# Second attention: each tile's probabilities scaled by the row's reciprocal on GpSimd, ahead of the transposes

## The chip, the cores and the metric

One core of one Trainium2 chip. The metric is the device time of the whole kernel in microseconds (us), median over runs. Before the change it is 2228.61 us (three runs, 2228.41 to 2229.06).

## The reference, cut to what matters

The kernel computes two transformer blocks of two layers each over 512 latent rows (and 256 context rows in the first block). The change touches one stage, the multi-head latent attention of the first block's second layer:

```python
s = (jnp.einsum('bqhd,bkhd->bhqk', qn_b, kn_all)
     + jnp.einsum('bqhr,bkr->bhqk', qr_b, kr_all)).astype(jnp.float32) * scale
p = jax.nn.softmax(s, axis=-1).astype(dt)
return jnp.einsum('bhqk,bkhd->bqhd', p, v_all)
...
y = (o * jax.nn.silu(g)) @ w_o
```

There are 16 heads, 512 queries, 768 keys (512 latent and 256 context), 96 numbers per query and key and 64 per value. The softmax divides each query's exponentials by their sum. That division can be made on the probabilities, or on the output after the product with the values.

## The kernel before, in words

Everything is float32. A projection's operands are split in a high and a low part and cost three products (L365 to L367, split_product). The programs of the five engines are written out by hand; they meet at semaphores: Signal.mark numbers an instruction's increment, and wait_ge on the same key waits for it. Each engine runs its program in the order written, so an instruction that waits holds everything behind it on its engine.

**The attention's steps.** ATT_B (L1213) has 16 jobs, one per head, of four tiles of 128 queries by 768 keys: 64 tiles. A step t of the loops att_pe, att_dve, att_act and att_pool handles tile t, and the later work of earlier tiles. Within step t:
- TensorE (att_pe, L656) makes the scores of tile t (six products, L543, into two of four PSUM banks; it first waits for the exponential of tile t-2, which read those banks), then transposes the probabilities of tile t-2 (six, L615, in two lots of three, each into one of three turning banks), then prep_pe (up-projections of a later head's keys and queries), then its share of the value products of a finished pair of heads (L651), then, once per pair, the spread (below).
- VectorE (att_dve, L673) takes the negated row maximum of tile t (L553), copies the first lot of transposes of tile t-2 from PSUM to PT (L633), makes the reciprocals of a pair (L584), the pair's output (keep_o, b_keep, L1050), and the low parts of a later head's keys and queries (prep_dve: L1150, L1156, L1159, and for some heads rope products L820 to L829).
- ScalarE (att_act, L692) copies the second lot of tile t-2 (L635), makes the exponential of tile t with its row sums (L568, into PB and SUM), then high parts.
- GpSimd (att_pool, L711) gates a pair (L720, below) and makes the high and low parts of finished outputs (b_parts_pool, L1063: a cast L1068 and a subtraction L1070 per pair of heads). These stand at three steps only, named by pairs_at (L1220): pairs 0 and 1 at tile 3 of head 13, pairs 2 and 3 at tile 3 of head 14, pairs 4 to 6 at tile 2 of head 15. At the last pair's spread step, low_at, it first makes the low parts of three weight panels (split_low, L1481).

**How a pair is placed.** finish_att (L788) counts from z, the last tile of an odd head: its reciprocals at z+2, its spread at z+3, its value products in four shares at z+3 to z+6, its output at z+7 (for the last pair all value products at z+3, the output at z+4).

**The normalization before the change.** The probabilities stay unnormalized. att_spread (L586) multiplies each reciprocal column, broadcast, with the identity, so that the reciprocals of a pair lie along the free dimension of a PSUM bank (8 products, L594, recorded as 16). ScalarE copies that to BC (L604). GpSimd multiplies the gate by BC (L720, `gated`), and VectorE's output (L1053) is the value product times that gate; it waits for `gated`.

The steps have different lengths, since only some carry the extra work. I call a pair's even head e and its odd head o, with tiles 0 to 3: e2, e3, o0 and o1 are long (value products, up-projections), o2, o3, e0 and e1 are short (scores and transposes alone). Lines above are those of the kernel before.

## Time and profile before

| | |
|---|---|
| median of 3 runs | 2228.61 us |
| span of the profiled execution | 2224.4 us |
| the profiled execution's own time | not given apart from its span; the runs lie 4.2 us above the span |
| TensorE matmuls busy over the span | 94% |
| VectorE, ScalarE, GpSimd busy over the span | 47%, 40%, 34% |
| mean granted TensorE clock | 0.971 of full |
| the second attention | about 592 us to 808 us of the span |

The span runs from the first to the last instruction. Busy shares are means over stages with different limits. In a timeline row the first number is the start (us from the span's start), the second the duration, and brackets at the end tell how long the engine was idle before and what ended it. In --lines style rows the numbers behind the bar are the busy time of the group (us) and the mean of one (ns), then the idle time before them. TensorE's clock has two levels, 2.4 GHz (1.00) and 1.2 GHz (0.50).

### The profile page before, as it was taken

The page shows a single profiled execution, that of the slowest core. Times are in us where ns is not written, and L with a number is a line of the kernel's source. Part 1 is how long each engine was busy: PE and PEld are TensorE (multiplying, and loading weights), DVE is VectorE, ACT ScalarE, POOL GpSimd, SP SyncE. Part 2 cuts the span into 40 slices and gives each one's busy share as a digit, 9 for nine tenths or more (in the row PEclk, how much of TensorE's full clock was granted, in tenths as well). Part 3 has the DMA queues.
Part 4 walks back from the last instruction along what each step waited for, and adds up shares of the span by engine and source line. Part 5 has one row for each costly group of instructions (what it writes and reads, how often), then busy time and mean ns, then how long its engine had stood idle before and what let it go on. Part 6 is the DMA issues. An engine that isn't in the chain of part 4 may idle for free.

```text
span 2224.4 us, 30049 instructions
## 1 busy us (share of the span) xinstructions
PE 2087.9 (94%) x11530; PEld 1654.5 (74%) x11530; DVE 1040.3 (47%) x1723; ACT 891.2 (40%) x1645; POOL 755.4 (34%) x446
## 2 busy tenths in 40 slices
PE   5999999999999999998889999998998889999997
PEld 4888655788666667986667888886986677888886
DVE  3520887422466632388337344333127625625253
ACT  4322666423566643535433222234127633322222
POOL 1331122343000153330344444453445453444443
PEclk9999999999999999799899999999999999999999
DMA  7221333132000012220122333332321132333332
GB/s 284 67 65 57 108 96 96 48 104 67 19 1 1 1 58 76 58 85 20 53 70 86 104 95 95 95 95 76 94 87 39 28 96 60 102 96 98 100 92 69
DMA packets 255890, 169.17 MB, mean 76 GB/s; under 512 B 5776, under 2 KB 247159, under 8 KB 254599
## 3 DMA queue, kind: packets, MB, share of 16 engines
q1 hardware_dynamic: 252512, 158.55, 24.0%
q0 software_dynamic: 2192, 8.45, 1.2%
q8 instruction: 94, 1.54, 0.3%
q10 hardware_dynamic: 1047, 0.26, 0.1%
q14 instruction: 45, 0.37, 0.1%
HBM read 165.10 MB, written 2.14 MB: 75 GB/s over the span
## 4 chain that ended last, share of the span: by engine, by line
PE 82%; DVE 8%; issue 4%; ACT 3%; POOL 1%; DMA 0%; ACTq 0%; DVEq 0%; POOLq 0%
PE ps L365 21%; PE ps L366 20%; PE ps L367 20%; PE ps L543 6%; PE ps L651 5%; PE ps L615 3%; PE ps L594 1%; DVE MX L556 1%; DVE PT L633 1%; POOL WL L1481 1%; PE ps L516 1%; DVE NB L553 1%; PE ps L987 1%; ACT PB L568 1%; PE ps L1086 1%
## 5 line engine op out<-in xcount | busy, mean ns | idle before, releaser
L1481 POOL TENSOR_TENSOR WL<-raww,WH 128x1024 fp32r<-128x1024 f32 (+2 forms) x247 | 581.8, 2360 | 894.2 <-ACT WH L317 882.7
L365 PE MATMUL ps<-HH,WH 128*128 128x512 f32 (+1 forms) x1368 | 526.0, 384 | 29.1 <-DVE HL L486 17.0
L366 PE MATMUL ps<-HL,WH 128*128 128x512 f32 (+1 forms) x1368 | 520.7, 381 | 0.0
L367 PE MATMUL ps<-HH,WL 128*128 128x512 f32 (+1 forms) x1368 | 519.7, 380 | 0.0
L317 ACT ACTIVATE WH<-raww 128x1024 fp32r<-128x1024 f32 (+2 forms) x247 | 254.2, 1035 | 327.7 <-PE ps L367 327.6
L365 PEld LDWEIGHTS ps<-HH,WH 128*128 128x128 f32 x1368 | 260.9, 191 | 88.8 <-issue 29.9
L367 PEld LDWEIGHTS ps<-HH,WL 128*128 128x128 f32 x1368 | 260.4, 190 | 49.3
L366 PEld LDWEIGHTS ps<-HL,WH 128*128 128x128 f32 x1368 | 261.0, 191 | 46.6
L568 ACT ACTIVATE PB<-ps,NB 128x256 f32<-128x256 f32 (+5 forms) x256 | 167.8, 656 | 101.8 <-DVE NB L557 51.9
L615 PE MATMUL ps<-ident,PB 128*128 128x128 f32 x952 | 154.5, 278 | 11.6 <-DVE PT L633 7.1
L651 PE MATMUL ps<-PT,ARENA 128*64 128x512 f32 (+3 forms) x688 | 132.8, 493 | 11.2 <-ACT PT L635 7.8
L365 PE MATMUL ps<-f_h,WH 128*128 128x512 f32 x352 | 137.7, 391 | 1.6 <-DVE f_l L2605 1.6
L367 PE MATMUL ps<-f_h,WL 128*128 128x512 f32 x352 | 137.1, 389 | 0.0
L366 PE MATMUL ps<-f_l,WH 128*128 128x512 f32 x352 | 137.0, 389 | 0.0
L553 DVE TENSOR_REDUCE NB<-ps 128x1 f32<-128x768 f32 (+4 forms) x128 | 92.5, 722 | 94.5 <-PE ps L543 92.8
L615 PEld LDWEIGHTS ps<-ident,PB 128*128 128x128 f32 x952 | 108.7, 142 | 22.0 <-DVE PT L633 12.6
L635 ACT ACTIVATE PT<-ps 128x256 f32<-128x256 f32 (+1 forms) x192 | 83.5, 435 | 90.3 <-PE ps L615 88.2
L2418 DVE TENSOR_TENSOR ARENA<-ps,ARENA 128x512 f32<-128x512 f32 x60 | 40.8, 689 | 157.8 <-PE ps L367 131.1
L2592 DVE SCALAR_TENSOR_TENSOR ARENA<-ARENA,COL 128x511 f32<-128x511 f32 x44 | 110.8, 2518 | 1.6
L2181 ACT ACTIVATE ARENA<-ARENA 128x512 f32<-128x512 f32 x44 | 27.9, 633 | 172.9 <-DVE ARENA L2594 172.9
L556 DVE TENSOR_REDUCE MX<-ps 128x1 f32<-128x512 f32 (+3 forms) x128 | 74.0, 578 | 42.0 <-PE ps L543 41.5
L633 DVE COPY PT<-ps 128x384 f32<-128x384 f32 (+2 forms) x192 | 91.2, 475 | 3.2 <-PE ps L615 2.1
(330 smaller groups left out, 3392.0 us busy)
## 6 DMA issues: line engine op xcount, KB each, us to landing
raww<-in_ffn_w_up SPq DMA_DIRECT2D x88, 512.0 KB, 3.8
raww<-in_ada_w SPq DMA_DIRECT2D x32, 512.0 KB, 3.6
raww<-in_ffn_w_down SPq DMA_DIRECT2D x32, 448.0 KB, 3.7
raww<-in_odd_w_in SPq DMA_DIRECT2D x24, 512.0 KB, 3.7
raww<-in_even_w_in SPq DMA_DIRECT2D x21, 512.0 KB, 3.7
raww<-in_a_w_in SPq DMA_DIRECT2D x20, 512.0 KB, 3.8
raww<-in_ffn_w_down SPq DMA_DIRECT2D x16, 512.0 KB, 3.8
ADA<-in_ada_w SPq DMA_DIRECT2D x6, 1024.0 KB, 16.9
```

The lines of the kernel that those rows point to most:

```text
L317: nc.scalar.activation(parts_of(k)[0], raw_slot(k), ACT.Copy).then_inc(*split_hi.mark(k))
L365: nc.tensor.matmul(out, lh, rh, start=start and k == ks[0], stop=False)
L366: nc.tensor.matmul(out, lh, rl, start=False, stop=False)
L367: ins = nc.tensor.matmul(out, ll, rh, start=False, stop=stop and k == ks[-1])
L543: ins = nc.tensor.matmul(ps[:, bk, c0 % 512:c0 % 512 + w], lhs, rhs, start=(q == 0), stop=(q == len(ms) - 1), skip_group_check=True)
L553: nc.vector.tensor_reduce(nb, score_span(A, r, i), AX_X, ALU.max, negate=True)\
L568: nc.scalar.activation(PB[:, t % 4, 0:job["tiles"][i]["n"] * P], score_span(A, r, i), ACT.Exp, bias=NB[:, r % 4, i:i + 1], scale=A["scale" ...
L615: ins = nc.tensor.transpose(ps[:, b, q * P:(q + 1) * P], PB[:, t % 4, (first + q) * P:(first + q + 1) * P], ident[:, :])
L633: nc.vector.tensor_copy(dst, src).then_inc(*pt_dve.mark(*key))
L651: ins = nc.tensor.matmul(ps[p0:p0 + HD, 7, a:z], v, PT[at][:, blk, q0_ + a:q0_ + z], start=(q == 0), stop=(q == n - 1), skip_group_check=True)
L1481: nc.gpsimd.tensor_tensor(lo, raw_slot(k), hi.bitcast(F32), ALU.subtract).then_inc(*split_lo.mark(k))
L2592: chain(dve, dve_step, nc.vector.scalar_tensor_tensor(c[:, 1:S], u[:, 0:S - 1], col(cw, 22 + m), c[:, 1:S], ALU.mult, ALU.add))
```

## The change

For ATT_B alone ("weigh": True), in four parts. VectorE makes one reciprocal of 128x1 per tile (tile_rcp), in the step after the tile's own, right behind that step's maximum. GpSimd multiplies the tile's probabilities in PB, 128x768, in place by that column (tile_weigh), first in its step. TensorE's transposes of the tile wait for that product (`weighed`) instead of the exponential. The pair reciprocals, the spread products, their copy to BC and the gate's multiplication are left out, and b_keep no longer waits for `gated`. The split_low of the last spread step stays, and pairs_at is unchanged.

```diff
+        def tile_rcp(dve, A, r, i):
+            dve.wait_ge(*exp_made[A["name"], r, i])
+            nc.vector.reciprocal(RCP[:, r % 4, i:i + 1], SUM[:, r % 4, i:i + 1])\
+                .then_inc(*rcp_made.mark(A["name"], r, i))
+
+        def tile_weigh(pool, A, r, i):
+            t = A["at"](r, i)
+            p = PB[:, t % 4, 0:A["jobs"][r]["tiles"][i]["n"] * P]
+            pool.wait_ge(*rcp_made[A["name"], r, i])
+            nc.gpsimd.tensor_scalar(p, p, RCP[:, r % 4, i:i + 1], None, ALU.mult)\
+                .then_inc(*weighed.mark(A["name"], r, i))
...
         def att_turn(pe, A, r, i):
             t = A["at"](r, i)
-            pe.wait_ge(*exp_made[A["name"], r, i])
+            pe.wait_ge(*(weighed if "weigh" in A else exp_made)[A["name"], r, i])
...
-                if t in A["spread_at"]:
+                if t in A["spread_at"] and "weigh" not in A:
                     att_spread(pe, A, A["spread_at"][t])
...
                 if r is not None:
                     att_max(dve, A, r, i)
+                if "weigh" in A and att_at(A, t - 1)[0] is not None:
+                    tile_rcp(dve, A, *att_at(A, t - 1))
                 q, j = att_at(A, t - 2)
                 if q is not None:
                     att_keep("dve", A, q, j)
-                if t in A["rcp_at"]:
+                if t in A["rcp_at"] and "weigh" not in A:
                     att_rcp(dve, A, A["rcp_at"][t])
...
-                if t in A["spread_at"]:
+                if t in A["spread_at"] and "weigh" not in A:
                     att_spread_keep(act, A, A["spread_at"][t])
...
         def att_pool(pool, A):
             for t in range(A["steps"]):
+                if "weigh" in A and att_at(A, t - 1)[0] is not None:
+                    tile_weigh(pool, A, *att_at(A, t - 1))
                 if t in A["spread_at"]:
...
                         split_low(pool, A["low_at"][t])
+                if t in A["spread_at"] and "weigh" not in A:
                     pool.wait_ge(*bc_made[A["name"], q])
...
         def b_keep(dve, job, r):
             g = b_gate(job)
-            dve.wait_ge(*gated["B", r])
...
-        ATT_B = finish_att({"name": "B", "jobs": b_jobs(), "scale": 1.0, "keep_o": b_keep, "gate": b_gate,
+        ATT_B = finish_att({"name": "B", "weigh": True, "jobs": b_jobs(), "scale": 1.0, "keep_o": b_keep, "gate": b_gate,
```

## Rows read from the trace of the kernel before

**Rows 1.** The page's part 1: busy time, share of the span, instructions.

```profile
PE 2087.9 (94%) x11530; PEld 1654.5 (74%) x11530; DVE 1040.3 (47%) x1723; ACT 891.2 (40%) x1645; POOL 755.4 (34%) x446
```

**Rows 2.** Windows, second attention: length; PE, PEld, DVE, ACT, POOL busy (instructions); PEclk; DMA share, GB/s.

```profile
590.00:816.00 226.00, 211.01 (x1193) 139.10 (x1192) 139.01 (x213) 144.56 (x283) 30.34 (x25) 0.99 0.03 8
```

**Rows 3.** Waits, 620 to 830 us: who waited for whom, total us, times, longest.

```profile
PE ps L543 <- DVE b_ql L1159: 5.2, 6, 0.9
...
DVE ARENA L1053 <- POOL ARENA L720: 11.5, 1, 11.5
```

**Rows 4.** Groups by line and shape, 592 to 808.3 us, TensorE and ScalarE.

```profile
L594 PE MATMUL ps<-ident,RCP 128*64 128x128 f32 x128 | 8.6, 275 | 0.0
...
L568 ACT ACTIVATE PB<-ps,NB 128x768 f32<-128x768 f32 x64 | 57.5, 898 | 15.2 <-DVE NB L553 14.7
...
L568 ACT ACTIVATION_READ_ACCUMULATOR PB<-ps,NB 128x1 f32 x64 | 12.6, 198 | 0.0
```

**Rows 5.** Timeline of TensorE, 740 to 760 us: the steps o3 to e3 of one pair.

```profile
745.77 0.48 PE L543 MATMUL ps<-b_kk,b_qh 96*128 96x512 f32 x1
...
748.60 0.47 PE L543 MATMUL ps<-b_kk,b_qh 96*128 96x512 f32 x1 [0.87 <-DVE b_ql L1159]
...
749.74 0.82 PE L615 MATMUL ps<-ident,PB 128*128 128x128 f32 x6
750.61 0.47 PE L543 MATMUL ps<-b_kk,b_qh 96*128 96x512 f32 x1
...
752.32 0.48 PE L543 MATMUL ps<-b_kk,b_qh 96*128 96x512 f32 x1
...
753.46 0.82 PE L615 MATMUL ps<-ident,PB 128*128 128x128 f32 x6
...
755.98 1.04 PE L594 MATMUL ps<-ident,RCP 128*64 128x128 f32 x16
756.96 0.50 PE L543 MATMUL ps<-b_kk,b_qh 96*128 96x512 f32 x1
```

**Rows 6.** Timeline of VectorE, 740 to 757 us.

```profile
748.49 0.96 DVE L553 TENSOR_REDUCE NB<-ps 128x1 f32<-128x768 f32 x1
...
751.95 0.96 DVE L553 TENSOR_REDUCE NB<-ps 128x1 f32<-128x768 f32 x1 [0.59 <-PE ps L543]
...
753.28 0.19 DVE L584 RECIPROCAL RCP<-SUM 128x8 f32<-128x8 f32 x1
753.51 0.95 DVE L1150 TENSOR_TENSOR b_kk<-ARENA,b_kk 64x768 fp32r<-64x768 f32 x1
```

**Rows 7.** Groups by line and shape of GpSimd, whole span.

```profile
L379 POOL TENSOR_TENSOR ACC<-ACC,SQ 128x768 f32<-128x768 f32 x5 | 9.2, 1846 | 20.7 <-ACT SQ L396 20.7
L1070 POOL TENSOR_TENSOR b_ol<-ARENA,b_oh 128x512 fp32r<-128x512 f32 x7 | 8.9, 1276 | 0.6
...
L1068 POOL CAST b_oh<-ARENA 128x512 fp32r<-128x512 f32 x7 | 4.3, 610 | 9.1 <-issue 5.6 <-DVE ARENA L1053 3.2
L959 POOL CAST a_oh<-ARENA 128x256 fp32r<-128x256 f32 x7 | 2.8, 396 | 34.8 <-DVE ARENA L937 30.0 <-DVE MROW L1015 4.8
```

**Rows 8.** GpSimd's casts of L1303: shortest, median and longest duration in ns.

```profile
L1303 POOL CAST o_oh<-OT x7: 609/1055/1055, 1686.9 to 1772.2; 128x512 fp32r<-128x512 f32 x7
```

**Rows 9.** Timeline, 786 to 830 us: the attention's end, all engines.

```profile
790.31 1.94 PE L651 MATMUL ps<-PT,ARENA 128*64 128x512 f32 x8
...
792.17 0.50 PE L543 MATMUL ps<-b_kk,b_qh 96*128 96x512 f32 x1
...
800.36 7.07 PE L651 MATMUL ps<-PT,ARENA 128*64 128x512 f32 x24 [1.86 <-ACT PT L635]
...
808.23 0.50 PE L365 MATMUL ps<-b_oh,WH 128*128 128x512 f32 x1
```

**Rows 10.** Windows of 2 us, TensorE alone: length, busy (instructions), granted clock, DMA share, GB/s.

```profile
798.00:800.00 2.00, 0.50 (x5) 1.00 0.00 0
...
802.00:804.00 2.00, 2.00 (x7) 0.50 0.76 223
```

More of the change, by code:

```diff
@@ L189, in build @@
             scores_made turned pv_made max_made exp_made sink_made rcp_made
-            pt_dve pt_act o_made spread_made bc_made gated summed act_step dve_step pool_step const_made""".split()
+            weighed pt_dve pt_act o_made spread_made bc_made gated summed act_step dve_step pool_step const_made""".split()
         sg = {n: signal(n) for n in names}
@@ L193, in build @@
          pool_out, squared, rms_made, diag_made, h_made, x_made, scores_made, turned,
-         pv_made, max_made, exp_made, sink_made, rcp_made, pt_dve, pt_act, o_made,
+         pv_made, max_made, exp_made, sink_made, rcp_made, weighed, pt_dve, pt_act, o_made,
          spread_made, bc_made, gated, summed,
```

## The prediction

> **What bounds the kernel now.** I read the page's busy shares first: TensorE is busy 94% of the span and no other engine half of it [rows 1]. Then the windows of the second attention: TensorE is busy 211 of 226 us, VectorE and ScalarE about 140, GpSimd 30, at a clock of 0.99 [rows 2]. So the stage is TensorE's queue, with GpSimd nearly free. The waits show the exceptions: six times TensorE waits 0.9 us for VectorE's low parts of the next head (5.2 us together), and once, at the end, VectorE waits 11.5 us for GpSimd's gate [rows 3]. The timeline of TensorE then gives the steps of one pair: o3 starts at 745.77, e0 at 748.60, e1 at 750.61, e2 at 752.32, e3 at 756.96 [rows 5]. The question is whether the new chain (maximum, reciprocal, GpSimd, transpose) fits in short steps: o3 to e0 is 2.8 us, e0 to e1 2.0, e1 to e2 1.7, and only e2 to e3 is long, 4.6.
>
> **What is removed.** The spread is 128 recorded products, one group per pair; a group holds TensorE from 755.98 to 756.96, 0.98 us [rows 4, 5]. Eight groups are 7.8 us, all on TensorE's path. The copy to BC and the gate's multiplication go too; ScalarE and GpSimd had room for them, so I take nothing for that. The 11.5 us wait at the end frees nothing: TensorE went straight on to the output projection at 808.23 and did not wait for that output [rows 3, 9].
>
> **What one weighing costs.** No row shows GpSimd multiplying by a column. Below stands its cast, one stream in and one out: 396 ns for 256 elements and 610 ns for 512, so 0.836 ns an element and 182 ns fixed, 0.82 us for 768. Above stands its two-input addition of 128x768, 1.85 us [rows 7]. The multiplication also reads one stream, so I stay near the cast and take 1.0 us. Each hand-over between engines I take as 0.1 us, and the reciprocal, by the 128x8 one, from its start at 753.28 to the next instruction at 753.51, as 0.2 us [rows 6]. In all 64 weighings add 64 us of GpSimd to 30; it does not become a full engine. Latency is the matter.
>
> The Trainium skill, GPSIMD Engine Reference, section Engine selection, says to keep elementwise work on VectorE, with one-input work on GpSimd "roughly line-rate"; the casts' 0.836 ns an element agree. Its section Elementwise — side-by-side cycle accounting gives 1.8 cycles an element at 1.2 GHz for a tight loop, an estimate of 1.15 us for 768; by that the sum below would be 3 us more.
>
> **One transition of pairs, worked out on the rows.** In o2 VectorE now has a reciprocal more (0.2), and its low parts with two operands from memory meet a weighing (I take 0.2 more; one-sided slowdowns of that sort are seen on GpSimd, 609 against 1055 ns for one cast [rows 8]). e0 was released by those low parts, so it starts at 749.0 instead of 748.60, and the maximum of tile o3 at 748.9, ending at 749.85. Only behind it comes the reciprocal of tile o2, to 750.0; GpSimd weighs 750.15 to 751.15; the transposes of o2 start at 751.25. TensorE would be ready 1.14 us after its scores started (748.60 to 749.74 [rows 5]), at 750.14: a stall of 1.1 us. e1 starts 0.57 later, at 751.8, and was at 750.61. Tile o3's weighing is ready at 752.7, TensorE at 752.95: no stall. e2 starts at 753.5. The maximum of e1 starts 1.34 us after its scores (750.61 to 751.95 [rows 5, 6]), 753.15, ends 754.1; reciprocal of e0 to 754.25; weighing to 755.4; transposes at 755.5, while TensorE is ready at 754.65: a stall of 0.85. From these transposes to e3 it was 3.5 us (753.46 to 756.96), without the spread 2.5: e3 starts at 758.0 instead of 756.96. The long steps e3, o0, o1 have over 3.5 us, in which the chain fits. So one transition, with its spread already taken off, is 1.05 us longer. The exponential is not the end of the chain: 0.90 plus 0.20 us behind a maximum [rows 4] is done before the next tile's maximum is. Three of the seven transitions also hold rope work on VectorE ahead of a maximum; the same steps give 1.5 there. Sum: 4 x 1.05 + 3 x 1.5 = 8.7 us. The head of the attention adds 0.3.
>
> **The casts that stand before weighings.** GpSimd's high and low parts, 610 + 1276 ns and gaps, are 2.0 us a pair of heads [rows 7]. They used to run in an idle engine; now the next tile's weighing is queued behind them, and TensorE's transposes behind that. Two pairs at tile 3 of head 13: the weighing of that tile ends 4.1 us later, in a short step: 3.4 us of stall instead of 0.9, plus 2.5. Two pairs at tile 3 of head 14, in long steps: plus 1.0. Three pairs at tile 2 of head 15, last steps: tile 62's weighing starts 9.7 us after step 62's scores, 6.1 of them the casts; transposes of 62 at 10.8 and of 63 at 11.9; then ScalarE's weight copy and its last lot, value products at about 13.6, where before they started 8.2 us after 792.17 (at 800.36) [rows 9]. That is 5.4 later, less the last spread, 1.0: plus 4.4.
>
> **The clock.** The end of the attention shows what a hole does: TensorE busy 0.50 of 2 us at 798, then the granted clock at 0.50 (1.2 GHz) at 802 [rows 10]. One fall there cost 1.3 us: the 24 value products took 7.07 us, where 8 undisturbed ones take 1.94 [rows 9], so 5.8 for 24. The new hole of 3.4 us should cost the same; the one of about 6 us starts the fall that is there already earlier and lets it catch more, for which I take 1.0: plus 2.3.
>
> **Sum.** 8.7 + 0.3 + 2.5 + 1.0 + 4.4 + 2.3 = 19.2 us on a span of 2224.4, so 2243.6; the median of the runs, 2228.6, lies 4.2 above the span, so 2248. Per microsecond of weighing the sum moves by 19 (two stalls in each of seven transitions, and the ends): the cast's 0.82 gives 15.8 and 2244, the addition's 1.85 gives 35.4 and 2264.
>
> **Rivals.**
> - **The weighing hides and the spreads are a gain.** For it: GpSimd idles and 7.8 us of TensorE work go. It needs stalls below the spread, which by the slope of 2 per transition means a weighing under 0.5 us, less than GpSimd's own cast of 512 elements [rows 7]. If the reciprocals also overlapped the maxima, 7.8 us less: 2221. Decides at the transposes of o2 and e0: no idle before them. Chance 0.05; that both just cancel, 2228.6, also 0.05.
> - **GpSimd multiplies at the pace of its two-input addition**, 1.85 us: 2264. For it: that is the only arithmetic of this size in the rows. Chance 0.10.
> - **VectorE and GpSimd hold each other up.** Four low-part instructions with two operands in memory lie in each head; the cast that goes from 609 to 1055 ns [rows 8] shows 0.45 us. On every weighing that is 0.45 x 19 = 8.5 us more: 2256.5. Chance 0.08. The Trainium skill, SBUF — State Buffer, section Who interferes with whom, says that the second of two such instructions fully blocks until the first ends, not that both slow; by that rule only the weighings that start second pay, which is nearer to my 0.2.
> - **The clock falls in every transition**, not at the two holes alone. There TensorE would idle some 2.5 us in about 8. At 1.3 us a fall, as above, 7 x 1.3 = 9 more, 2257. Against it: the same stretch today has stalls of 0.9 and the stage's clock is 0.99 [rows 2]. Chance 0.10.
>
> **How the numbers follow.** My forecast has 0.62. I give 2248 with 2236 to 2267: the low end is the cast's price (15.8) without the clock's losses (2.3), the casts' delays in head 13 and 14 (3.5) and half of the end's cost (2.2), the high end is just past the addition's price. About 0.2% (4.5 us) is what a measurement here tells from no change. Faster 0.05, within 0.05, slower 0.90.
>
> **What would show it.** Right: the weighing's mean near 1.0 us; TensorE idle before L615-type transposes, released by GpSimd, about twice per transition and near 1 us each, 25 us in all with 3 us at head 13's last tile and 6 us at the end; the stage from 216 to about 235 us, all other stages unchanged. Wrong: a weighing outside 0.8 to 1.9 us; releases by GpSimd in the long steps as well; a gap at the end under 3 us; or a difference in any stage outside 592 to 830 us.

## The result, and the profile after

The changed kernel takes 2278.4 us (median of 4 runs, 2265.2 to 2279.1) against 2228.5 for the kernel before in the same batch: a ratio of 1.0215 [1.0201, 1.0229]. The direction was right and the size was not: 49.9 us slower where 19.4 were forecast, and outside the range. The changed kernel has two levels of time, 2265 and some 2278; the profiled execution is the single one at 2265 (span 2263.4), and experiment 11 below shows where the other 12 us lie.

The page's part 1 of the changed kernel answers [rows 1]: GpSimd has 131 us more, TensorE 5 us more although 128 products are gone.

```profile
PE 2092.6 (92%) x11402; PEld 1653.0 (73%) x11402; DVE 1064.1 (47%) x1779; ACT 888.0 (39%) x1637; POOL 886.8 (39%) x502
```

The stage first. I measure the second attention from its first score product to the first product of its output projection: 592.28 to 808.23 before, 595.80 to 859.40 after. These are the windows of the changed kernel (length; PE, PEld, DVE, ACT, POOL busy; granted clock), first the attention, then a stretch of the next layer's row products:

```profile
595.80:859.40 263.60, 215.02 (x1029) 140.08 (x1029) 158.39 (x262) 136.73 (x268) 160.97 (x81) 0.88 0.02 7
946.00:976.00 30.00, 30.00 (x257) 30.00 (x257) 15.28 (x17) 20.08 (x35) 9.92 (x4) 1.00 0.29 86
```

The same window of the kernel before (592.28 to 808.23) is 215.95 us long with TensorE busy for 202.13, at a clock of 0.99 ([rows 2] is the same stretch with some us on each side). So the attention is 47.6 us longer. Everything ahead of it is 3.5 us longer and everything behind it 12.2 us shorter in this profile, both of which vary from execution to execution of these kernels as well. Read TensorE's column: busy 202.1 became 215.0, and idle (length less busy) 13.8 became 48.6. Of the busy time the spreads took 7.8, so the same products cost 20.7 us more than before, at a mean clock of 0.88 instead of 0.99. The account of the stage is then **34.8 us of new idle time, 20.7 us by which products take longer at the lower clock, 7.8 us of spreads gone**: 47.7. It is an account of TensorE's time and not yet of causes: a product that runs slower can fill what would otherwise be a wait.

The weighing itself, from the groups by line (busy us, mean ns, idle before), and the waits from 590 to 870 us (total us, times, longest):

```profile
L596 POOL TENSOR_SCALAR PB<-PB,RCP 128x768 f32<-128x768 f32 x64 | 141.0, 2205 | 128.2 <-DVE RCP L588 127.8
```

```profile
POOL PB L596 <- DVE RCP L588: 127.8, 56, 33.3
...
PE ps L628 <- POOL PB L596: 46.8, 30, 7.4
```

The multiplication takes 2.2 us, more than the highest bound of the forecast. And nearly all of TensorE's idle time, 46.8 of 48.6 us, ends with GpSimd's weighing; before, the waits were other and smaller ones [rows 3].

TensorE's timeline of one pair transition, heads 9 to 10, from the scores of tile o3 at 741.13. It is one of the three with rope work:

```profile
741.13 0.48 PE L543 MATMUL ps<-b_kk,b_qh 96*128 96x512 f32 x1
...
744.14 1.53 PE L628 MATMUL ps<-ident,PB 128*128 128x128 f32 x6 [1.72 <-POOL PB L596]
...
747.90 0.88 PE L628 MATMUL ps<-ident,PB 128*128 128x128 f32 x6 [0.31 <-POOL PB L596]
...
751.11 0.87 PE L628 MATMUL ps<-ident,PB 128*128 128x128 f32 x6 [1.28 <-POOL PB L596]
...
753.71 0.87 PE L628 MATMUL ps<-ident,PB 128*128 128x128 f32 x6 [0.68 <-POOL PB L596]
```

Four transposes in a row wait, where I expected two. The first of them also runs at 1.2 GHz: six transposes in 1.53 us, against 0.88. The transition of [rows 5], heads 11 to 12, has no rope work. In the changed kernel its o3 starts at 770.76:

```profile
770.76 0.47 PE L543 MATMUL ps<-b_kk,b_qh 96*128 96x512 f32 x1
...
773.77 0.87 PE L628 MATMUL ps<-ident,PB 128*128 128x128 f32 x6 [1.73 <-POOL PB L596]
...
777.40 1.54 PE L628 MATMUL ps<-ident,PB 128*128 128x128 f32 x6 [1.16 <-POOL PB L596]
...
784.28 0.87 PE L628 MATMUL ps<-ident,PB 128*128 128x128 f32 x6 [1.23 <-POOL PB L596]
```

The waits of the transposes of o2 and e0 are there, 1.16 and 1.23 us where the forecast had 1.1 and 0.85, and so is the forecast's free passage of o3. The new one, 1.73 us, is that of tile o1: its transposes stand in step o3, but its reciprocal comes behind the maximum of o2, and step o2 is short. From o3 to e3 the transition takes 16.20 us instead of 11.19. GpSimd in the stretch of the first view (start, duration, idle before) has no gap as long as a weighing:

```profile
745.64 2.20 POOL L596 TENSOR_SCALAR PB<-PB,RCP 128x768 f32<-128x768 f32 x1 [1.55 <-DVE RCP L588]
748.85 2.20 POOL L596 TENSOR_SCALAR PB<-PB,RCP 128x768 f32<-128x768 f32 x1 [1.01 <-DVE RCP L588]
751.45 2.21 POOL L596 TENSOR_SCALAR PB<-PB,RCP 128x768 f32<-128x768 f32 x1 [0.40 <-DVE RCP L588]
```

The loop reads off: a weighing ends (747.84), the transposes start (747.90), the scores behind them follow (748.54), their maximum comes behind rope work in VectorE's queue and runs to 751.3, the reciprocal behind it frees the weighing at 751.45, the second after the one that the loop began with. The engines take turns where they used to overlap.

The end of the attention, TensorE only, answers [rows 9]:

```profile
814.31 1.54 PE L628 MATMUL ps<-ident,PB 128*128 128x128 f32 x6 [2.78 <-POOL PB L596]
...
831.33 0.87 PE L628 MATMUL ps<-ident,PB 128*128 128x128 f32 x6 [3.12 <-POOL PB L596]
...
846.99 1.54 PE L628 MATMUL ps<-ident,PB 128*128 128x128 f32 x6 [7.38 <-POOL PB L596]
849.17 1.54 PE L628 MATMUL ps<-ident,PB 128*128 128x128 f32 x6 [0.64 <-POOL PB L596]
851.39 8.05 PE L664 MATMUL ps<-PT,ARENA 128*64 128x512 f32 x24 [0.67 <-ACT PT L648]
859.37 0.50 PE L365 MATMUL ps<-b_oh,WH 128*128 128x512 f32 x1
```

There are three holes behind casts: 2.8 us at head 13's last tile (forecast 3.4), 3.1 at head 14's last tile, where the forecast had only 1.0 more, and 7.4 at the end (forecast about 6). The last 24 value products run at the lower clock again, 8.05 us.

The length of the attention by place, from the starts of the scores in TensorE's timelines (us more than in the kernel before; runs 3 and 5 are described below):

| place | forecast | run 3, weighing 1.24 us | run 5, 2.20 us, holes filled | changed kernel |
|---|---|---|---|---|
| first scores to o3 of head 1 | 0.3 | 0.4 | 2.7 | 4.7 |
| six transitions, o3 to e3, heads 1 to 12 | 7.65 | 4.9 | 17.7 | 21.9 |
| the stretches between them, e3 to o3 | 0 | -0.1 | -0.1 | -0.1 |
| o3 of head 13 to the output projection | 11.25 | 10.6 | 20.4 | 21.1 |
| sum | 19.2 | 15.8 | 40.7 | 47.6 |

So the loss lies where the forecast put it, and the long steps take part in none of it.

### The profile page after: what moved, and what is told of

Its sections match the earlier page's. It is cut to its first block, busy times and chain, and to the rows that moved or that the text cites. A ratio compares the mean times of both kernels' runs of the same rounds, so it can differ in the third digit from the quotient of the medians.

```text
span 2263.4 us, 29870 instructions
## 1 busy us (share of the span) xinstructions
PE 2092.6 (92%) x11402; PEld 1653.0 (73%) x11402; DVE 1064.1 (47%) x1779; ACT 888.0 (39%) x1637; POOL 886.8 (39%) x502
## 4 chain that ended last, share of the span: by engine, by line
PE 80%; DVE 8%; issue 5%; POOL 4%; ACT 3%; DMA 0%; ACTq 0%; DVEq 0%; POOLq 0%
PE ps L365 20%; PE ps L366 20%; PE ps L367 20%; PE ps L543 6%; PE ps L664 5%; PE ps L628 3%; POOL PB L596 2%; DVE MX L556 1%; PE ps L607 1%; DVE NB L553 1%; POOL WL L1498 1%; DVE PT L646 1%; PE ps L516 1%; PE ps L1005 1%; PE ps L1103 1%
## 5 line engine op out<-in xcount | busy, mean ns | idle before, releaser
L628 PE MATMUL ps<-ident,PB 128*128 128x128 f32 x952 | 164.7, 293 | 54.5 <-POOL PB L596 46.8
L596 POOL TENSOR_SCALAR PB<-PB,RCP 128x768 f32<-128x768 f32 x64 | 141.0, 2205 | 128.2 <-DVE RCP L588 127.8
L628 PEld LDWEIGHTS ps<-ident,PB 128*128 128x128 f32 x952 | 114.6, 150 | 70.9 <-POOL PB L596 53.8
L646 DVE COPY PT<-ps 128x384 f32<-128x384 f32 (+2 forms) x192 | 91.1, 475 | 22.8 <-PE ps L628 21.5
```

The lines of the kernel that those rows point to most:

```text
L596: nc.gpsimd.tensor_scalar(p, p, RCP[:, r % 4, i:i + 1], None, ALU.mult)\
L628: ins = nc.tensor.transpose(ps[:, b, q * P:(q + 1) * P], PB[:, t % 4, (first + q) * P:(first + q + 1) * P], ident[:, :])
L646: nc.vector.tensor_copy(dst, src).then_inc(*pt_dve.mark(*key))
```

## Experiments

Runs of one batch share the runs of the kernel before (2227.2 to 2228.5), and each ratio is against those. For the attention alone I give, from the window of each profile, its length, TensorE's busy and idle time, and the granted clock.

**1. The price alone.** The kernel before, with five GpSimd instructions added at its very end, on 256, 512 and 768 elements, one after the other.

```
+            for n in (256, 512, 768):
...
+                        ins = nc.gpsimd.tensor_copy(o, x)
...
+                        ins = nc.gpsimd.tensor_scalar(o, x, c, None, ALU.mult)
...
+                        ins = nc.gpsimd.tensor_scalar(o, x, 0.5, None, ALU.mult)
...
+                        ins = nc.gpsimd.tensor_tensor(o, x, c.to_broadcast([P, n]), ALU.mult)
...
+                        ins = nc.gpsimd.tensor_tensor(o, x, BENCH[:, 0:n], ALU.mult)
```

> The kernel before, with five GpSimd operations on idle memory added behind its last work, each waited for before the next, at 256, 512 and 768 elements: cast-like copy, multiplication by a column, multiplication by a constant, product with a broadcast column, product of two tiles. Theory L (the operation itself is slow): the column multiplication of 768 takes 2.2 us here too, with VectorE nearly idle. Rival C (VectorE held it up in the attention): here it takes under 1.3 us, near the copy's 0.8. If the constant's form is fast and the column's slow, it is the column operand that costs.

2236.7 us in one run. The timeline of GpSimd; the other engines are still at work up to 2224.2 and done behind it:

```profile
2212.20 0.93 POOL L1481 TENSOR_SCALAR BENCH<-BENCH,RCP 128x256 f32<-128x256 f32 x1
...
2216.23 1.56 POOL L1481 TENSOR_SCALAR BENCH<-BENCH,RCP 128x512 f32<-128x512 f32 x1
...
2224.99 2.20 POOL L1481 TENSOR_SCALAR BENCH<-BENCH,RCP 128x768 f32<-128x768 f32 x1
2227.28 2.13 POOL L1483 TENSOR_SCALAR BENCH<-BENCH 128x768 f32<-128x768 f32 x1
2229.49 1.47 POOL L1485 TENSOR_TENSOR BENCH<-BENCH,RCP 128x768 f32<-128x768 f32 x1
2231.04 1.47 POOL L1487 TENSOR_TENSOR BENCH<-BENCH 128x768 f32<-128x768 f32 x1
```

So 2.2 us is the operation's own price: it is the same with VectorE idle, and nearly the same with a constant in the place of the column. It grows by 2.48 ns an element ((2.20 - 0.93) us / 512), the cast by 0.84 [rows 7]. That VectorE makes it dear is refuted. The form with two inputs, one of them the column repeated, is a third cheaper, 1.47 us. Three of the fifteen instructions are out of line: the constant on 512 elements 2.15 us (2.13 on 768), the product of a tile with itself on 512 1.90 (1.47 on 768), the copy of 768 1.70 (0.61 for 512). All three ran beside VectorE's last four products of two operands in memory, here from 2217.39 to 2224.21, so VectorE can hold GpSimd up, though the two-input form on 512 ran there undisturbed (1.04 us); it does not do so to the weighing, which takes 2.20 us in the kernel too.

**2. Neither the spreads nor the weighing**: the normalization is left out altogether.

```
-            pe.wait_ge(*(weighed if "weigh" in A else exp_made)[A["name"], r, i])
+            pe.wait_ge(*exp_made[A["name"], r, i])
...
-                    tile_rcp(dve, A, *att_at(A, t - 1))
...
-                    tile_weigh(pool, A, *att_at(A, t - 1))
```

> The changed kernel without weighing and without tile reciprocals: transposes wait for the exponential, and nothing normalizes the probabilities (that division is left out). What the removal alone is worth. Theory L: the eight spreads' 7.8 us of TensorE come off in full, 2221. Rival: part of them covered waits of other engines, and under 4 us come off, 2225 or more.

2222.3 us (9 runs), 0.9977 [0.9967, 0.9987]. Attention 209.3, busy 194.4, idle 14.8, clock 0.99. What the change removes is worth 5.0 us in the time and 6.7 in the stage, of the 7.8 forecast. So the new chain costs 54.3 us of stage in the changed kernel.

**3 and 4. The same chain with a shorter weighing**: only 384 or only 32 of each row's 768 probabilities are multiplied; the rest stays unnormalized.

```
-            p = PB[:, t % 4, 0:A["jobs"][r]["tiles"][i]["n"] * P]
+            p = PB[:, t % 4, 0:3 * P]        (run 3)
+            p = PB[:, t % 4, 0:32]           (run 4)
```

> The changed kernel, weighing only the first 384 of 768 columns (the other half stays unnormalized). The weighing should take about 1.2 us instead of 2.2. Theory L with 19 us per us of weighing: 19 us off, about 2259 from 2278, and most idle time before the transposes goes. Rival K (the granted clock's falls make most of the loss): it stays above 2268 as long as holes are there at all.

> The changed kernel, weighing 32 of 768 columns: the same chain of engines with an operation of about 0.25 us. Theory L: no stall in the transitions, the casts in front of weighings still cost some us; 7.8 us of spreads are gone, so 2224 to 2232. Rival H (the hand-overs and the place behind the maximum cost as much as the multiplication): 2240 or more.

Run 3: 2245.6 (5 runs, 2232 to 2249), 1.0071 [1.0047, 1.0095]. That is 33 us off where 19 were expected: more than the weighing's slope comes back. Run 4: 2232.2 (10 runs), 1.0024 [1.0015, 1.0034], at the upper end of what was expected. First the group and the waits of run 3, then those of run 4:

```profile
L596 POOL TENSOR_SCALAR PB<-PB,RCP 128x384 f32<-128x384 f32 x64 | 79.6, 1244 | 160.4 <-DVE RCP L588 160.1
```

```profile
PE ps L628 <- POOL PB L596: 31.6, 28, 6.4
```

```profile
L596 POOL TENSOR_SCALAR PB<-PB,RCP 128x32 f32<-128x32 f32 x64 | 23.2, 363 | 202.3 <-DVE RCP L588 202.0
```

```profile
PE ps L628 <- POOL PB L596: 13.5, 12, 5.5
```

| weighing, us | attention | TensorE busy | TensorE idle | clock |
|---|---|---|---|---|
| none (run 2) | 209.3 | 194.4 | 14.8 | 0.99 |
| 0.36 (run 4) | 221.1 | 199.3 | 21.7 | 0.97 |
| 1.24 (run 3) | 231.8 | 198.1 | 33.7 | 0.98 |
| 2.20 (changed kernel) | 263.6 | 215.0 | 48.6 | 0.88 |

The idle column is nearly a straight line: 13.6 us per us of weighing from 0.36 to 1.24 ((33.7 - 21.7) / 0.88), 15.5 from there to 2.20 ((48.6 - 33.7) / 0.96). The busy column is flat up to 1.24 us and then jumps by 17. The length, which is what counts, does not follow one slope: 12 us per us of weighing up to 1.24, 33 from there. The profile of run 3 is of its quickest execution (2232); like the changed kernel's it has the clock at 1.00 in the next layer's row products, and the 11 to 16 us to its other runs fit the 12.5 of run 11 below; none of those was profiled.

**5. Is it the clock?** The holes of the changed kernel are filled: ahead of the wait for the weighing, in four of the eight steps of a pair, TensorE transposes the identity 8 times into the bank that it is about to use.

```
-            pe.wait_ge(*(weighed if "weigh" in A else exp_made)[A["name"], r, i])
...
+                if g == 0 and "weigh" in A and (r % 2, i) in ((1, 1), (1, 2), (1, 3), (0, 0)):
+                    for q in range(8):
+                        nc.tensor.transpose(ps[:, b, (q % 4) * P:(q % 4 + 1) * P], ident[:, :], ident[:, :])
+                if g == 0:
+                    pe.wait_ge(*(weighed if "weigh" in A else exp_made)[A["name"], r, i])
```

> The changed kernel, and TensorE fills its holes: for the tiles whose transposes stand in short steps (o1, o2, o3, e0) it makes eight transposes of the identity into the same bank before it waits for the weighed tile. 256 transposes of about 0.11 us more work. Theory K (the holes make the granted clock fall, and the falls cost as much as the holes): the time at 0.50 inside the attention, 54 us in the changed kernel, falls below 20, and the attention gets shorter than 263.6 us by 5 or more in spite of the added work. Theory L alone (the clock's falls lie in waiting time and cost little): 263.6 us or more.

2267.6 us (4 runs), 1.0184 [1.0169, 1.0199], 10.8 below the changed kernel. Its attention:

```profile
591.40:848.10 256.70, 225.85 (x1284) 155.28 (x1284) 158.26 (x262) 136.53 (x268) 160.77 (x81) 0.97 0.02 5
```

TensorE does 256 transposes more, and the attention is 6.9 us shorter. The clock is 0.97 instead of 0.88: worked out from these means, some 15 us at the lower level instead of 63. The 256 are 34.2 us by their group; that leaves 191.7 for the kernel's own products, no more than in runs 2 to 4. So the jump of 17 us in busy time is the clock's, and it came from the holes. In length it is worth 6.9 us and not 17, since products that run slower fill waits. The transition shown above can be compared with the same one in the second profile of the changed kernel (run 11), where the clock did not fall in it:

```profile
740.74 0.87 PE L628 MATMUL ps<-ident,PB 128*128 128x128 f32 x6 [1.71 <-POOL PB L596]
...
744.49 0.87 PE L628 MATMUL ps<-ident,PB 128*128 128x128 f32 x6 [1.84 <-POOL PB L596]
...
747.71 0.87 PE L628 MATMUL ps<-ident,PB 128*128 128x128 f32 x6 [1.31 <-POOL PB L596]
...
750.30 0.87 PE L628 MATMUL ps<-ident,PB 128*128 128x128 f32 x6 [0.67 <-POOL PB L596]
```

With the fall the second wait is 0.31 us instead of 1.84, and from o3 to e3 it is 15.26 us with it and 15.25 without. In the transitions without rope work a fall cost more or less by where it came: heads 11 to 12 take 16.20 us with one and 14.66 in run 5, heads 7 to 8 take 14.69 with one.

**6. The cheaper form of the same multiplication.**

```
-            nc.gpsimd.tensor_scalar(p, p, RCP[:, r % 4, i:i + 1], None, ALU.mult)
+            nc.gpsimd.tensor_tensor(p, p, RCP[:, r % 4, i:i + 1].to_broadcast([P, 6 * P]), ALU.mult)
```

> The changed kernel, the weighing written as a two-input product with the reciprocal column broadcast, which took 1.47 us for 768 elements where the column multiplication took 2.20 (measured alone at the kernel's end). Theory L, by the run with 384 columns (1.24 us, 2246): 1.5 us should give 2248 to 2258. Rival C (two reading streams meet VectorE's two-input operations): the operation takes 1.8 us or more in the attention and the time stays above 2262.

2257.7 us (4 runs, 2253 to 2265), 1.0138 [1.0117, 1.0160]; the weighing takes 1466 ns, as in run 1. Attention 249.8, busy 206.5, idle 43.3, clock 0.94. Of 20.8 us gained by the median, 13.8 show in this profile's attention (the profile is of the slowest of the four runs). The idle time fell by 5.3 only, not by 0.74 x 15.5 = 11.5. VectorE's busy time in the stage rose from 158.4 to 171.5 with the same 262 instructions: here the two-input form did slow VectorE. How much of the gain that took is not measured.

**7. The casts spread out**: GpSimd's high and low parts, one pair per step instead of two or three.

```
-        ATT_B["pairs_at"] = {ATT_B["at"](13, 3): (0, 1), ATT_B["at"](14, 3): (2, 3), ATT_B["at"](15, 2): (4, 5, 6)}
+        ATT_B["pairs_at"] = {ATT_B["at"](13, 1): (0,), ATT_B["at"](13, 2): (1,), ATT_B["at"](14, 0): (2,),
+                             ATT_B["at"](14, 2): (3,), ATT_B["at"](15, 0): (4,), ATT_B["at"](15, 1): (5,), ATT_B["at"](15, 3) + 1: (6,)}
```

> The changed kernel with the output casts of the seven pairs spread: one pair each at tiles 1 and 2 of head 13, 0 and 2 of head 14, 0 and 1 of head 15, the last behind the last weighing. The prediction put 7.9 us on their old places (2.5, 1.0, 4.4) and 2.3 on the clock there: 7 to 12 us off, about 2268 of 2278, and no gap over 4 us before the last transposes. Rival: the gaps move into other steps and less than 3 us come off.

2253.7 us (4 runs, 2250 to 2264), 1.0125 [1.0099, 1.0151]. Attention 255.5, idle 42.4, clock 0.91. The waits from 595 to 850 us:

```profile
PE ps L628 <- POOL PB L596: 40.6, 30, 2.5
```

As many waits, 30, the longest 2.5 us instead of 7.4. The stage is 8.1 us shorter, and 9.3 from o3 of head 13 on, where the casts were; the forecast had 7.9 for the casts (2.5 + 1.0 + 4.4) and 2.3 for the clock at the same holes. This step of the prediction holds in its sum. The median fell by 24.7, more than that; its profile shows no stretch at the lower clock in the next layer's row products, unlike the level at 2278, so about 12 us of the 24.7 belong to that (run 11).

**8. Another place for the factor.** VectorE multiplies the identity by the reciprocal (128x128) and TensorE transposes by a product with that diagonal; GpSimd does nothing.

```
+            nc.vector.tensor_scalar(DIAG[:, A["at"](r, i) % 3, :], ident[:, :], RCP[:, r % 4, i:i + 1], None, ALU.mult)\
+                .then_inc(*weighed.mark(A["name"], r, i))
...
+                    if "weigh" in A:
+                        ins = nc.tensor.matmul(ps[:, b, q * P:(q + 1) * P],
+                                               PB[:, t % 4, (first + q) * P:(first + q + 1) * P], DIAG[:, t % 3, :],
+                                               start=True, stop=True)
+                        continue
```

> Normalization at no width: VectorE makes the reciprocal and then a 128x128 diagonal of it (identity times the column), and TensorE turns each block by a product with that diagonal instead of a transpose. No spread, no weighing, no gate product, GpSimd free again. Theory L: the chain behind the maximum is two short VectorE operations, 0.3 to 0.4 us, no stall before the turns; the spreads' 5 to 7 us come off, 0.2 to 0.4 us per head come back on VectorE: 2222 to 2228. Rival H (any work between the exponential and the transpose costs more than the spread): above 2232. If a real product with 128x128 is slower than a transpose, the 384 turns show it.

2255.2 us (4 runs), 1.0128 [1.0111, 1.0145]. The stalls are gone: idle 7.5 us, half of run 2's, clock 1.00. But TensorE's busy time is 234.7, 40.2 more than in run 2. Groups by line:

```profile
L592 DVE TENSOR_SCALAR DIAG<-ident,RCP 128x128 f32<-128x128 f32 x64 | 20.4, 319 | 2.3
...
L633 PE MATMUL ps<-DIAG,PB 128*128 128x128 f32 x768 | 97.2, 276 | 4.0 <-DVE DIAG L592 3.6
```

There are 768 records for 384 products: a true fp32 product is recorded twice where a transpose is recorded once, and costs about twice. That the latency makes the stalls is right, but this way out is dear: against the changed kernel the attention is 21.4 us shorter, against the kernel before 26.2 longer. The 2222 to 2228 that I expected missed the price of the product.

**9. More distance.** The transposes and the copies behind them come three steps after the scores instead of two (there are four buffers of probabilities).

```
-                q, j = att_at(A, t - 2)
+                q, j = att_at(A, t - A.get("lag", 2))        ("lag": 3 in the second attention)
```

> The changed kernel with one line of distance more: transposes and their copies of tile t-3 instead of t-2 in step t, value products and outputs one step later. The weighing (2.2 us) and the casts' places are as changed. Theory L (the loss is the latency between a maximum and the transposes two steps on): with a third step the chain, 2.33 + 0.3 + 2.2 + 0.1 us, fits in two steps of 3.7 us or more, short of 1.2 us here and there; the transition stalls mostly go, the casts' and the end's stay: 2235 to 2250. Rival M (GpSimd's amount of work, not its place, is the limit, 141 us of weighing and 20 of casts and panels in a stage of 216): the loss stays near the changed kernel's, above 2262.

2239.5 us (4 runs), 1.0059 [1.0046, 1.0072]. Attention 228.7, busy 203.2, idle 25.4, clock 0.95. The waits of the stage:

```profile
PE ps L628 <- POOL PB L596: 12.5, 6, 6.5
```

GpSimd does the same 64 weighings at 2.2 us (busy 162.9), and TensorE waits for them 6 times instead of 30. So the amount of GpSimd's work never was the matter, its place in the chain was.

**10. All three together**: 6, 7 and 9.

> As the run before, with the weighing as a product with the broadcast column (1.47 us) and the casts one pair at a time. Theory L: no stall left in the transitions, some 3 us more at the end, the spreads' 5 to 7 us off: 2222 to 2230, so level with the kernel before or just under it. Rival M: 2240 or more.

2233.6 us (12 runs, 2224 to 2237), 1.0025 [1.0015, 1.0036], above the 2222 to 2230 expected. Attention 223.4, idle 20.9, clock 0.97. What TensorE waits for now:

```profile
PE ps L628 <- DVE PT L646: 11.0, 12, 1.7
...
PE ps L628 <- POOL PB L596: 2.2, 3, 1.1
```

The weighing is hidden, and the next engine shows itself: VectorE, whose copies of the transposed probabilities come late behind the maximum and the reciprocal, at 174.6 us busy of 223.4.

**11. The changed kernel once more**, for a profile of its other level.

> The changed kernel once more. Its four runs were 2265.2 and three near 2278.5. Theory G: the 13 us are the granted clock in the stretch of the next layer's row products, 75 to 125 us behind the attention: in the profiled 2265 it stayed at 1.00, in the kernel before it is at 0.50 for 23.9 us. If this run is near 2278, its profile shows about 24 us at 0.50 there and the rest of the kernel behind the attention takes 1416 us, if near 2265, none and 1404.

2274.5 us in one run. Its windows, against the two of the section above:

```profile
592.80:856.00 263.20, 214.15 (x1028) 139.16 (x1028) 158.93 (x262) 136.51 (x268) 160.79 (x81) 0.90 0.02 6
944.00:974.00 30.00, 30.00 (x175) 30.00 (x175) 12.00 (x16) 9.17 (x16) 4.74 (x2) 0.65 0.17 51
```

The attention is the same to 0.4 us. Behind it, TensorE is busy all of the 30 us in both profiles, but does 175 products here and 257 there, at a clock of 0.65 against 1.00. What follows the attention takes 1416.5 us here and 1404.0 there; before it took 1416.2, with the lower clock in that stretch too (0.72 from 900 to 930). So 12.5 us of the difference between profiles lie outside the attention. The profiles of these experiments are of the same two kinds: behind the attention come 1404 us in three of them (the changed kernel, runs 3 and 7) and 1415 to 1417 in runs 2, 4 to 6, 8 to 14 and the kernel before. Why the clock stays low there in most executions and not in all, no run shows.

**12. The multiplication on VectorE**, behind the reciprocal, and nothing on GpSimd.

```
-            nc.gpsimd.tensor_scalar(p, p, RCP[:, r % 4, i:i + 1], None, ALU.mult)
+            nc.vector.tensor_scalar(p, p, RCP[:, r % 4, i:i + 1], None, ALU.mult)
```

> The changed kernel with the weighing on VectorE, behind the tile's reciprocal: one 128x768 multiplication by a column, about 0.5 to 0.9 us (a 128x128 one took 0.29). GpSimd is free, no casts in the way. Theory L: 0.9 us against 2.2 less one hand-over removes most stalls in front of transposes, but VectorE gets 64 x 0.7 = 45 us more in its queue, which sets the start of e0 and the rope pairs: 2232 to 2245, far under the changed kernel's 2278.

2234.7 us (8 runs, 2232 to 2248), 1.0048 [1.0029, 1.0066]. Group by line:

```profile
L596 DVE TENSOR_SCALAR PB<-PB,RCP 128x768 f32<-128x768 f32 x64 | 43.9, 687 | 2.3
```

VectorE does in 0.69 us what takes GpSimd 2.20. The profile is of an execution at 2248 (attention 236.0, busy 211.2, idle 24.8, clock 0.93); which stretch those at 2232 save was not profiled. It shows that the sum of idle time does not set the clock: with 24.8 us of it the clock is at 0.93 here, with 33.7 in run 3 and 28.9 in run 14 it is at 0.98. With nothing else altered the median is 43.8 us faster than the changed kernel, though its 43.9 us stand on the busier engine.

**13. Run 10 with the copies first**: on VectorE the copy of the transposed tile goes ahead of the reciprocal.

> As the run with the third step, the broadcast product and the casts apart (2233.6), with one order turned on VectorE: the copy of the turned lot stands before the tile's reciprocal. Theory W (what is left there is a new wait: 20 us in which TensorE waits before transposes for VectorE's copy of the lot before, which now stands behind a maximum and a reciprocal): most of these waits shrink by the 0.2 us of the reciprocal or more, 2 to 4 us off, 2229 to 2232. Rival: the copy waits for the same maximum as before, the weighing comes 0.5 us later, and the time stays or rises, 2233 to 2238.

2232.4 us (10 runs, 2220 to 2238), 1.0009 [0.9992, 1.0027], level with the kernel before. That is 1.2 us under run 10, between what the theory and the rival asked for, and decides nothing. The waits for VectorE's copies fell from 11.0 to 6.3, those for GpSimd rose from 2.2 to 4.8, as the order of the two says.

**14. Run 12 with the third step of distance.**

> The third step of distance, with the weighing on VectorE (0.69 us each, 44 us more in its queue) and GpSimd free. If latency before the transposes was what was left of the loss in the run with the weighing on VectorE (stalls of 23 us there, 2234.7), it goes: 2224 to 2229, level with the kernel before or under it. If VectorE's queue itself is the new bound (it sets the start of e0, the copies and the maxima), the time stays at 2231 or more.

2242.4 us (6 runs, 2231 to 2244), 1.0057 [1.0039, 1.0076], no better than run 12: what was expected if VectorE's queue is the new bound. The waits from 590 to 840 us:

```profile
PE ps L628 <- DVE PT L646: 22.8, 26, 2.6
```

With the weighing in VectorE's queue the copies wait behind it, whatever the distance. None of these versions beats the kernel before except run 2, which leaves the work out.

## Why the prediction was wrong

**What held.** The stage and its bound; that the removed spreads are a gain (6.7 of 7.8 us in the stage); that the matter is the latency of a chain and not GpSimd's sum of work (run 9: same work, 35 us less); the places, with nothing lost in the long steps; that the casts queued ahead of weighings cost some 8 us, though head 14's hole was dearer than forecast (3.1 us of wait) and head 13's cheaper (2.8); and that nothing outside the attention changes: before and behind it the profiles differ by what executions of one kernel differ by (run 11). The sign of being wrong that the prediction named came true, a weighing outside 0.8 to 1.9 us.

**The step that failed** is the price of the weighing: "The multiplication also reads one stream, so I stay near the cast and take 1.0 us." It is 2.205 us in the kernel and 2.20 alone (run 1), above both bounds. The reasoning by streams picked the wrong neighbour twice: the cast at 0.82 us was no lower neighbour but another operation, and the two-input addition at 1.85 was no upper bound: multiplying by a scalar is slower on GpSimd than a product of two inputs (2.20 against 1.47). The Trainium skill, GPSIMD Engine Reference, section Engine selection, says that one-input work is roughly line-rate on GpSimd; this case's traces agree for casts (0.84 ns an element) and not for multiplying by a scalar (2.48 ns an element). The rival at the two-input pace had the mechanism of the result, with 1.85 us, and fell 14 us short. By the prediction's own slope the missing 1.2 us are 22.8: 42.0 us in the stage instead of 19.2.

**The second mis-sized term is the clock.** 2.3 us were forecast, for the two holes at the end, and none for the head and the transitions. There the clock did fall, in five of the six transitions of the changed kernel's profile. Run 5 gives what that costs, 6.9 us (4.2 in the transitions, 2.0 in the head, 0.7 behind): with the holes filled the clock is at 0.97 and the stage that much shorter despite 256 products more. The 20.7 us by which the products take longer are not the cost, since most of them run in what would be waits. The rival "the clock falls in every transition" had this mechanism, and 9 us for it. The argument against it was "the same stretch today has stalls of 0.9", and with stalls near 1 us (run 3, the longest in the six transitions 1.3) the clock does stay up. But it is no matter of the waits' length alone. In the changed kernel the falls came with waits of 1.7 us and up to four in a row, yet the transition of heads 7 to 8 fell at its first wait, that of heads 5 to 6 kept its clock with 1.70, 1.84, 1.31 and 0.69 us, and the one shown under run 5 fell in one execution and not in the other. What decides between them stays open.

**The slope was right on the average, and that is partly luck.** In the six transitions it is 2 us per us of weighing in the forecast; measured, 1.6 each from 0.36 to 1.24 us and 2.2 from there to 2.20 with the clock kept up (68.2, 76.7 and 89.5 us in runs 4, 3 and 5). At its own price the sum was too high: interpolated between runs 4 and 3, a weighing of 1.0 us would have given about 2242, an estimate, where 2248 was forecast. The transitions with rope work, put at 1.5 us, took 0.5 to 0.7 more than before in run 3. The forecast also missed that the transposes of o1 wait ("The long steps e3, o0, o1 have over 3.5 us, in which the chain fits"); that wait is 0.75 us in run 3 and takes the place of one of 0.87 that TensorE had for VectorE's low parts [rows 5].

**Together**, for the stage: forecast 19.2; price 1.2 x 19 = +22.8; the clock beyond the two holes of the forecast, +6.9; rest -1.3, from the slope that was too steep at first. That is 47.6. The median missed by 30.4 and the stage by 28.4; the 2 us between them are less than what the attention's start moves between executions (591 to 596 us).

**The other rivals.** "The weighing hides" needed under 0.5 us. Run 4, at 0.36, is 1.0024 over the kernel before, but in the six transitions it takes 68.2 us where the kernel before takes 71.9: there the weighing nearly hides (65.9 us in run 2) and the spreads are a gain. Of the 11.8 us of stage over run 2, 9.4 lie behind o3 of head 13, where the casts stand ahead of the weighings. "VectorE and GpSimd hold each other up" is refuted as a cost of the weighing (2.20 alone). Its count of four low-part instructions with two operands in each head is not what the rows say either: there are two and a cast, 16 of each. In the other direction it shows: VectorE's cast of 32x512, 0.42 us before, takes 0.90 and 1.01 beside weighings.

```profile
743.46 0.90 DVE L1176 CAST b_ql<-b_rl 32x512 fp32r<-32x512 f32 x1
...
755.87 1.01 DVE L1176 CAST b_ql<-b_rl 32x512 fp32r<-32x512 f32 x1
```

It is 23 us of VectorE's busy time in all (158.4 against 135.1, reciprocals of 10 us among it). The Trainium skill, SBUF — State Buffer, section Who interferes with whom, has one such instruction block until the other ends. For the casts the trace agrees: all 15 that start during a weighing end 0.26 to 0.28 us behind its end, however late they started, so they wait and are not slowed. VectorE's two-operand low parts do not wait for that end: those held up end 1.70 us (64x768) and 1.44 us (64x512) after the weighing's start. In run 6, where the weighing has two inputs, they do: those that start during a weighing end 0.80 and 0.54 us behind its end (means 1.79 and 1.37 us instead of 1.24 and 0.82), and the casts then come when the weighing is over and take 0.42 us.

## What to carry to other kernels

Price an operation on GpSimd by the same operation, not by one that reads as many streams: if no row shows it, the range must reach to several times the nearest one, and one instruction on an idle engine settles it. A new link in a chain that TensorE takes turns with costs its duration once per step in which there is no slack. Distance cures it (one more step between scores and transposes gave back 35 of 48 us of the stage, 39 of the median), and so does a shorter link (on VectorE 44 of the median, run 12); the two did not add up (run 14). For each step, ask which tile's link hangs on the step's end, as o1's hung on the short step o2. Stalls can bring the clock down too, but what slower products cost is read from the length of a stage, not from the engine's busy time: part of them runs in waits.

## What the runs showed of the hardware

On GpSimd, fp32, 128 partitions (run 1): multiplying 256, 512 and 768 elements by a column took 0.93, 1.56 and 2.20 us; the same result as a two-input product with the column broadcast 0.61, 1.04 and 1.47; a constant is hardly cheaper than a column (2.13). VectorE does the 768 in 0.69 (run 12). A GpSimd multiplication by a column holds VectorE's casts up to its own end, a GpSimd product of two inputs holds VectorE's two-operand instructions up to its end (changed kernel and run 6). VectorE's two-operand products held up GpSimd: its copy of 768 elements took 1.70 us beside them (run 1). On TensorE a true 128x128 fp32 product is recorded twice and costs about as much as two transposes (run 8: 40.2 us more for 384 of them). Some 30 holes, mostly of 1 to 2 us, went with a granted clock of 0.88 instead of 0.99 over a stretch of 264 us, and useless products in them brought it to 0.97 (run 5); the sum of idle time does not tell the clock (0.93 with 24.8 us in run 12, 0.98 with 33.7 in run 3), and the same holes brought it down in one execution and not in the next. And a stretch of TensorE work without holes can run at a clock of 0.65 in one execution and at 1.00 in the next of the same kernel, worth 12.5 us (run 11), so that a single profile of such a kernel may be off by a quarter of the effect that is looked for.
